# Two norms of a float32 transformer block: the first 128 tokens' tiles turned among the last output products, and two units begun ahead of the other tokens

## The reference

```python
def rmsnorm(x, w):
    y = x * lax.rsqrt(jnp.mean(x * x, axis=-1, keepdims=True) + EPS)
    return y * w

x = rmsnorm(x + (o * silu(gate)) @ odd_w_out, final_norm)   # end of first_block
h = rmsnorm(x, mix_norm);  proj = h @ w_mix_in              # 2048 -> 7184 columns, g_qkv first
...
x = x + attn @ w_xo                                         # the cross-attention's output
h = rmsnorm(x, ffn_norm);  u = causal_dwconv(h @ w_ffn_up, conv)
```

## Time and profile before

| | us |
|---|---|
| median of three runs | 2411.24 (2410.80 to 2411.55) |
| the profiled execution | 2411.45 |
| its span, first to last instruction | 2409.7 |
| PE busy | 2388.1 (99%) |
| PE weight loads busy | 2066.5 (86%) |
| DVE busy | 1629.7 (68%) |
| ACT busy | 1178.4 (49%) |
| weights read | 410.87 MB on the SP queue, 51.6% of the DMA engines' span |

### The profile page before, as it was taken

The page is one execution under the profiler, slowest core; times in us unless marked ns, Lnnn a source line. Parts: engine busy times, 40 slices in busy tenths (PEclk is TensorE's granted clock), DMA queues, the critical chain, the costliest instruction groups (busy, mean ns, idle before and its releaser), DMA issues.

```text
span 2409.7 us, 35511 instructions
## 1 busy us (share of the span) xinstructions
PE 2388.1 (99%) x14109; PEld 2066.5 (86%) x14109; DVE 1629.7 (68%) x2068; ACT 1178.4 (49%) x1439; POOL 157.9 (7%) x142
## 2 busy tenths in 40 slices
PE   8999999999999999999999999999999999999998
PEld 7888988898888888889988888988888888888887
DVE  6999776555685876696655446665777467755764
ACT  5433674544565654642654345545554334433433
POOL 1000000000200100000000000000212012200220
PEclk9999999999999999999999999999999999999999
DMA  8555546455436555553175555444565655555554
GB/s 251 189 195 186 164 140 214 147 180 171 158 108 207 166 183 177 183 167 106 37 253 176 199 186 164 141 175 161 190 203 179 208 175 194 189 194 191 183 180 143
DMA packets 337351, 422.45 MB, mean 175 GB/s; under 512 B 8494, under 2 KB 263228, under 8 KB 336716
## 3 DMA queue, kind: packets, MB, share of 16 engines
q1 hardware_dynamic: 334220, 410.87, 51.6%
q0 software_dynamic: 2544, 8.52, 1.1%
q10 hardware_dynamic: 464, 1.32, 0.2%
HBM read 418.53 MB, written 2.10 MB: 175 GB/s over the span
## 4 chain that ended last, share of the span: by engine, by line
PE 97%; DVE 1%; ACT 1%; DMA 0%; issue 0%; ACTq 0%; DVEq 0%
PE ps L759 36%; PE ps L760 18%; PE ps L816 10%; PE ps L818 10%; PE ps L817 10%; PE ps L763 1%; PE ps L764 1%; PE ps L762 1%; PE ps L1113 1%; PE ps L1105 1%; PE ps L1026 1%; PE ps L1030 1%; PE ps L855 0%; DVE h_cat L2343 0%; PE ps L1053 0%; DMA x<-in_x 0%
## 5 line engine op out<-in xcount | busy, mean ns | idle before, releaser
L759 PE MATMUL ps<-h_cat,w_hi 128*128 128x512 f32 x3824 | 1341.8, 396 | 5.4 <-DVE h_cat L2343 4.7
L760 PE MATMUL ps<-h_cat,w_lo 128*128 128x256 f32 x3824 | 1063.3, 278 | 0.0
L759 PEld LDWEIGHTS ps<-h_cat,w_hi 128*128 128x128 f32 x3824 | 717.0, 188 | 176.4 <-issue 8.3
L760 PEld LDWEIGHTS ps<-h_cat,w_lo 128*128 128x128 f32 x3824 | 719.4, 188 | 2.1 <-issue 1.9
L2200 DVE TENSOR_TENSOR w_lo<-ring,w_hi 128x2048 fp32r<-128x2048 f32 (+2 forms) x279 | 588.4, 2111 | 166.1 <-ACT w_hi L1417 163.1
L1417 ACT ACTIVATE w_hi<-ring 128x2048 fp32r<-128x2048 f32 (+2 forms) x279 | 493.0, 1767 | 87.6 <-PE ps L818 64.4
L2196 DVE TENSOR_TENSOR w_lo<-ring,w_hi 128x2048 fp32r<-128x2048 f32 (+1 forms) x136 | 302.8, 2232 | 231.2 <-ACT w_hi L1414 228.3
L1414 ACT ACTIVATE w_hi<-ring 128x2048 fp32r<-128x2048 f32 (+1 forms) x136 | 252.2, 1862 | 269.8 <-PE ps L818 239.6
L1435 ACT ACTIVATE stage<-ps 128x256 f32<-128x256 f32 x144 | 55.4, 384 | 400.1 <-PE ps L760 399.8
L816 PE MATMUL ps<-w_hi,h_cat 128*128 128x512 f32 x640 | 250.1, 391 | 0.0
L818 PE MATMUL ps<-w_hi,h_cat 128*128 128x512 f32 x640 | 249.2, 389 | 0.0
(11 more groups left out here) (466 smaller groups left out, 2335.2 us busy)
## 6 DMA issues: line engine op xcount, KB each, us to landing
ring<-in_w_ffn_up SPq DMA_DIRECT2D x44, 2048.0 KB, 8.0
ring<-in_w_mix_in SPq DMA_DIRECT2D x28, 2048.0 KB, 8.3
ring<-in_even_w_in SPq DMA_DIRECT2D x27, 2048.0 KB, 8.1
ring<-in_w_ffn_down SPq DMA_DIRECT2D x16, 2048.0 KB, 8.1
ring<-in_odd_w_in SPq DMA_DIRECT2D x11, 2048.0 KB, 9.3
ring<-in_even_w_out SPq DMA_DIRECT2D x8, 2048.0 KB, 8.2
ring<-in_odd_w_out SPq DMA_DIRECT2D x8, 2048.0 KB, 8.9
ring<-in_w_mix_out SPq DMA_DIRECT2D x8, 2048.0 KB, 8.2
```

The costliest lines, as they stand in the source:

```text
L759: mm(o[:, 0:2 * T], whi[slot][:, k, :], flat(cat[:, k]), start=first, stop=False)
L760: ins = mm(o[:, T:2 * T], wlo[slot][:, k, :], cat[:, k, 0, :], start=False, stop=end)
```

## The change

Behind norms 2 and 5 (`AHEAD`), and nowhere else:

- The eight transposes of the first tokens' first 1024 features move from behind the last output product to behind the second of the last four wide units of the second tokens.
- ACT, after the high parts of units 0 and 1, writes the first tokens' high parts of these eight tiles (`front_hi`, eight instructions of 128 columns), then unit 2's high part. DVE writes their low parts (`front_lo`, eight of 128 columns) after unit 0's low part.
- DVE makes unit 1's low part in two halves (`split_part`): contraction tiles 0 to 7 before `add_row`, which counts the new `lo_front`; tiles 8 to 15 behind the last `lo` of the norm, and only that counts `lo_ready`.
- PE, behind the last output product, runs `front_rows`: for units 0 and 1, eight matmuls each of the weights' high part with [high | low] of the first tokens (2 x 128 columns). Of the fillers three are left behind the mix norm and two behind the FFN norm, in other banks.
- Later `hi` and `lo` treat only the second tokens' 128 columns for pairs 0 to 3, and the first eight steps of units 0 and 1 multiply the high weights with the second tokens' 2 x 128 columns. Unit 1 starts on `lo_front` and waits for `lo_ready` at its ninth step.

The diff, without the list of semaphore names and most unchanged lines:

```diff
@@ -700,6 +700,9 @@
     HALVED = {1: 0, 2: 1, 5: 2}
+    AHEAD = {2: ("g_qkv", 0), 5: ("f_up0", 4)}
+    HALF_K = 8
+    FRONT, BACK = slice(0, P), slice(P, T)
@@ -728,7 +731,23 @@
-        def unit(g, j, n, i=None, rhs=None, tiles_ready=None, norm=None, read=None):
+        def two_of(o):
+            return o[:, 0:2 * T].rearrange("p (a t) -> p a t", a=2)
+        def front_rows(norm):
+            name, first = AHEAD[norm]
+            g = S[name]
+            pe.wait_ge(sem["half_ready"], first + 4)
+            for j in range(2):
+                before, at = seg_of_narrow[g.f0 + j - ACC]
+                pe.wait_ge(*emptied(before, at + 1))
+                pe.wait_ge(sem["hi_ready"], g.n0 + j + 1)
+                for k in range(HALF_K):
+                    mm(two_of(bank(g, g.n0 + j))[:, :, FRONT], whi[(g.n0 + j) % WHL][:, k, :], h_cat[:, k, :, FRONT],
+                       start=(k == 0), stop=False)
+        def unit(g, j, n, i=None, rhs=None, tiles_ready=None, norm=None, read=None, begun=None):
@@ -736,7 +755,11 @@
                 return
-            pe.wait_ge(*((sem["first_lo"], 1) if i is None and n == 0 else (sem["lo_ready"], k0 + 1)))
+            late_rest = begun is not None and j == 1
+            if late_rest:
+                pe.wait_ge(sem["lo_front"], AHEAD[begun][1] // 4 + 1)
+            else:
+                pe.wait_ge(*((sem["first_lo"], 1) if i is None and n == 0 else (sem["lo_ready"], k0 + 1)))
             if i is not None:
@@ -754,8 +777,13 @@
                         pe.wait_ge(sem["lo_ready"], 1)
+                if late_rest and step == HALF_K:
+                    pe.wait_ge(sem["lo_ready"], k0 + 1)
                 first, end = step == 0, step == g.kt - 1
-                if g.paired:
+                if begun is not None and step < HALF_K:
+                    mm(two_of(o)[:, :, BACK], whi[slot][:, k, :], cat[:, k, :, BACK], start=False, stop=False)
+                    ins = mm(o[:, T:2 * T], wlo[slot][:, k, :], cat[:, k, 0, :], start=False, stop=end)
+                elif g.paired:
                     mm(o[:, 0:2 * T], whi[slot][:, k, :], flat(cat[:, k]), start=first, stop=False)
@@ -780,7 +808,7 @@
                 unit(g, j, g.n0 + j, None, rhs, tiles_ready if j == 0 else None, norm if j == 0 else None,
-                     read if j == g.units - 1 else None)
+                     read if j == g.units - 1 else None, norm if norm in AHEAD and j < 2 else None)
                 if j == 0 and name in ("g_qkv", "x_k", "f_up0"):
@@ -821,7 +849,7 @@
-        def wide_seg(name, cat=None, tiles_ready=None, act0=None, first=0, norm=None, rows_apart=False, tile=None):
+        def wide_seg(name, cat=None, tiles_ready=None, act0=None, first=0, norm=None, rows_apart=False, tile=None, turned=None):
             g = S[name]
@@ -829,6 +857,9 @@
                         wide_unit(g, j, h_cat if cat is None else cat, tiles_ready, act0, (t,), tile=tile)
+                        if turned is not None and (t, j) == (1, g.units - 3):
+                            for p in range(4):
+                                turn_half(turned, p, 0).then_inc(sem["half_turned"], 1)
                 return
@@ -872,10 +903,13 @@
             if norm in HALVED:
-                for p in range(4):
-                    turn_half(norm, p, 0)
-                for n in range({1: 4, 2: 5, 5: 4}[norm]):
-                    mm(ps[n % 2][:, 0:T], ident[:], causal[:, 0:T], start=True, stop=True)
+                if norm in AHEAD:
+                    front_rows(norm)
+                else:
+                    for p in range(4):
+                        turn_half(norm, p, 0)
+                for n in range({1: 4, 2: 3, 5: 2}[norm]):
+                    mm(ps[n % 2 + (2 if norm in AHEAD else 0)][:, 0:T], ident[:], causal[:, 0:T], start=True, stop=True)
                 for p in range(4):
@@ -1092,7 +1126,7 @@
         pe.wait_ge(sem["masked"], A_ODD + DSA_HEADS)
-        wide_seg("o_out", tiles_ready=H_GROUPS["gate"], first=3, tile=gate_tile, rows_apart=True)
+        wide_seg("o_out", tiles_ready=H_GROUPS["gate"], first=3, tile=gate_tile, rows_apart=True, turned=2)
         turn_first(2)
@@ -1385,7 +1419,7 @@
         head_values(3)
-        wide_seg("x_out", tiles_ready=H_GROUPS["xattn"], first=2, rows_apart=True)
+        wide_seg("x_out", tiles_ready=H_GROUPS["xattn"], first=2, rows_apart=True, turned=5)
         turn_first(5)
@@ -1615,6 +1649,9 @@
             root_of(0, based, "half_std")
+            if k in AHEAD:
+                split_to(S[then].n0 + 2)
+                front_hi(k)
             split_to(S[then].n0 + 3)
@@ -1624,10 +1661,20 @@
             b = turned_tiles(k, p)
+            rows_ = slice(P if k in AHEAD and p < 4 else 0, T)
             for kk in range(2):
-                ins = af(h_hi[:, 2 * b + kk, :], turn_bank(k, p)[:, kk * T:(kk + 1) * T], ACT.Copy,
+                ins = af(h_hi[:, 2 * b + kk, rows_], turn_bank(k, p)[:, kk * T + rows_.start:(kk + 1) * T], ACT.Copy,
                          scale=col(NORMS[k], 2 * b + kk))
+        def front_hi(k):
+            for p in range(4):
+                act.wait_ge(sem["half_turned"], AHEAD[k][1] + p + 1)
+                for kk in range(2):
+                    ins = af(h_hi[:, 2 * p + kk, FRONT], turn_bank(k, p)[:, kk * T:kk * T + P], ACT.Copy,
+                             scale=col(NORMS[k], 2 * p + kk))
+                ins.then_inc(sem["half_hi"], 1)
@@ -1864,6 +1911,8 @@
         root_of(0, 3, "half_std", 1)
+        split_to(S["g_qkv"].n0 + 2)
+        front_hi(2)
         split_to(S["g_qkv"].n0 + 3)
@@ -2339,10 +2388,28 @@
             b = turned_tiles(k, p)
+            rows_ = slice(P if k in AHEAD and p < 4 else 0, T)
             for kk in range(2):
-                ins = stt(h_lo[:, 2 * b + kk, :], turn_bank(k, p)[:, kk * T:(kk + 1) * T], col(NORMS[k], 2 * b + kk),
-                          h_hi[:, 2 * b + kk, :].bitcast(F32), ALU.mult, ALU.subtract)
+                ins = stt(h_lo[:, 2 * b + kk, rows_], turn_bank(k, p)[:, kk * T + rows_.start:(kk + 1) * T], col(NORMS[k], 2 * b + kk),
+                          h_hi[:, 2 * b + kk, rows_].bitcast(F32), ALU.mult, ALU.subtract)
             ins.then_inc(sem["ht_ready"], 1)
+        def front_lo(k):
+            for p in range(4):
+                dve.wait_ge(sem["half_hi"], AHEAD[k][1] + p + 1)
+                for kk in range(2):
+                    ins = stt(h_lo[:, 2 * p + kk, FRONT], turn_bank(k, p)[:, kk * T:kk * T + P], col(NORMS[k], 2 * p + kk),
+                              h_hi[:, 2 * p + kk, FRONT].bitcast(F32), ALU.mult, ALU.subtract)
+                ins.then_inc(sem["half_ready"], 1)
+        def split_part(g, n, part_):
+            slot, c = n % WHL, g.c0 + (n - g.n0) // g.per_chunk
+            u0, k = ((n - g.n0) % g.per_chunk) * P, slice(8 * part_, 8 * part_ + 8)
+            dve.wait_ge(sem["hi_ready"], n + 1)
+            tt(wlo[slot][:, k, :], chunk(c % RING, g)[:, k, u0:u0 + P], whi[slot][:, k, :].bitcast(F32), ALU.subtract)\
+                .then_inc(sem["lo_ready" if part_ else "lo_front"], 1)
@@ -2392,7 +2459,12 @@
             scaled(k, x, 1)
-            split_to(S[then].n0 + 2)
+            if k in AHEAD:
+                split_to(S[then].n0 + 1)
+                front_lo(k)
+                split_part(S[then], S[then].n0 + 1, 0)
+            else:
+                split_to(S[then].n0 + 2)
             add_row(g, 1)
@@ -2415,6 +2487,10 @@
                 lo(k, b)
+            if k in AHEAD:
+                g = S[AHEAD[k][0]]
+                split_part(g, g.n0 + 1, 1)
+                st["split"] = g.n0 + 2
@@ -2724,7 +2800,9 @@
         scaled(2, x, 1)
-        split_to(S["g_qkv"].n0 + 2)
+        split_to(S["g_qkv"].n0 + 1)
+        front_lo(2)
+        split_part(S["g_qkv"], S["g_qkv"].n0 + 1, 0)
         add_row(S["o_out"], 1)
         two = lambda v: v.rearrange("p (a t) -> p a t", a=2)
```

More of the change, by code:

```diff
@@ L408, in build @@
              "row_ready", "emptied", "squared", "gained", "totalled", "std_ready", "rstd_ready", "scaled_dve", "scaled_act", "turned",
-             "scaled_one", "based", "half_std", "half_rstd", "ht_hi", "ht_ready", "tiles_read", "agate_read", "hhi_ready", "h_ready", "x_normed", "gain1_loaded", "gain_out_loaded",
+             "scaled_one", "half_turned", "half_hi", "half_ready", "lo_front", "based", "half_std", "half_rstd", "ht_hi", "ht_ready", "tiles_read", "agate_read", "hhi_ready", "h_ready", "x_normed", "gain1_loaded", "gain_out_loaded",
              "conv_tap", "bg_ready", "conv_total", "conv_mean", "conv_centred", "conv_sq", "conv_var", "conv_std", "conv_normed", "conv_silu",
```

## The result

The changed kernel takes 2422.3 us (median of five runs, 2421.97 to 2424.46) against 2411.55 us for the kernel before beside it (2410.80 to 2412.75): a ratio of 1.0046, with 95% between 1.0034 and 1.0059. It is slower by 10.8 us where 6.1 were forecast, and 0.3 us above the top of the predicted range. The profiled executions stand for this: spans of 2409.7 before and 2420.6 after, 10.9 more.

What follows compares the result with a forecast made beforehand. PE's chain bounds 97% of the span, so time is won only where PE idles or runs fillers. Stalls of 3.1 and 3.0 us, 6.1 together, on the median 2411.24 give 2417.3 us; range 2414.0 to 2422.0.

Steps and rivals of the forecast that it cites:

- The load behind the late half split: Load of units 4 and 5, issued 15 us later, delays unit 3: costs 3.1 us (mix norm) and 3.0 (FFN norm).
- The landing behind the mix norm: Load of units 4 and 5 takes the median 8.3 us from issue, landing at 809.6; earlier loads took 8.2 to 9.4.
- rival 2: ACT's table is loaded during the wait for the load: 1.28 us less at each norm, 2414.8 us; chance 0.20.
- The front parts: Work ahead of the first product and units 0 and 1: mostly hidden, each norm would win 1.0 us without the load.
- zero spare: DVE's low tiles and half split end at 788.3, when its add is due; at worst the add is 0.8 late.
- PE's gap ahead of the first product: Half as wide tiles behind the transposes save 0.4 us, so PE idles some 1.0 instead of 1.43.
- unit 1's 0.9: Eight steps of unit 1 shrink from 0.347 to 0.236 us; it runs free and gains the whole 0.9 us.
- The sum itself takes full speed: PE's clock in the stalls ahead of unit 3: the sum adds nothing for a fall to half speed.
- rival 3: The clock falls in a stall; one fall costs 2.8 us more, 2420, both at the upper end 2428; chance 0.12.
- The rows at the end: Clock falls between 2405 and 2406, over 3 us after PE's last matmul; a 3.8 us stall may or may not reach that.
- ACT's drains give the pitch of a unit: 5.54 us: Units of the loop behind the mix norm take 5.54 us each, 0.347 per step.
- rival 1: The late load is no bound and PE never waits for unit 1's bank; norms win 1.0 each: 2409.2; chance 0.07.

Runs made afterwards that it cites:

- experiment 1: Changed kernel with unit 1's low part made in one piece ahead of the last row's sum, so the load is on time: 2414.64 us, ratio 1.0014.
- experiment 2: Kernel before, with only the first load behind each norm waiting for one low part more: 2428.62 us, ratio 1.0072.
- experiment 5: Changed kernel, load still late, with ACT draining and DVE summing before they split in the two loops: 2415.52 us, ratio 1.0017.
- experiment 6: Experiment 4's kernel with the filler moved from behind unit 0 to behind unit 1: 2407.45 us; fillers at both: 2408.60; kernel before without filler: 2415.56.
- experiment 3: Changed kernel with ten fillers behind the mix norm and seven behind the FFN norm put ahead of unit 3: 2419.74 us, ratio 1.0034.
- experiment 4: Changed kernel with the second half split moved into DVE's gap behind the first scaling of the second tokens: 2413.63 us, ratio 1.0011.
- experiment 7: Experiment 1's kernel with the filler put behind unit 1 instead of unit 0: 2409.07 us, ratio 0.9990.
- experiment 8: Changed kernel with one more filler behind unit 3, of the mix loop (first kernel, 2422.63 us) or of both loops (second, 2422.82 us).

## Why the prediction was off, point by point

**Right: the direction and the mechanism.** "The load behind the late half split" happened at both norms as written: late count, late issue, ACT held in the split of unit 4 with its drain behind it, the sum late, PE idle ahead of unit 3, and no second stall. Experiments 1, 2 and 5 show the links: no late load, no stall; the late load alone, the stall; drain and sum ahead of the splits, none at unit 3.

**The terms of that step.** Against L', issue came at 12.8 and 12.0 (forecast 13.2 and 12.6). The landing behind the mix norm took 9.70, not 8.3, above the 9.4 at the top of the earlier trace rows; no run isolates why. Behind the FFN norm it took 8.2 (8.0). The table load did come after the landing, so rival 2 fell. Together unit 3 was 4.0 and 2.6 late, 6.6 for the 6.1 forecast. This term was sized well in sum, with a late landing at one norm against sooner issues at both.

**The front parts.** ACT's and DVE's narrow tiles took 0.27 each (2.16 and 2.17 for eight), not 0.30, and DVE stood 0.51 idle ahead of its add: "zero spare" was half a microsecond of spare. PE's gap ahead of the first product was 0.94 (1.0). Unit 0 ended at L' + 12.35, not 12.8, a gain of 0.6 rather than 0.1. With unit 1's 0.9 that makes about 1.5 a norm, 3.0 for two; experiment 6 collects 3.4.

**Wrong: the clock.** The step that failed is the clock in the stall, a term that the sum put at nothing: "The sum itself takes full speed", with a chance of 0.12 for rival 3. What the runs showed in its place: around waits of 4.90 and 3.64 us PE ran at half clock for 3.4 us each, 3.2 us together by the table. The rows at the end were read as leaving this open. A mean of 0.73 over the slice from 2405 puts the fall there near 2405.5, 3.6 us after PE's last matmul, and the stall forecast was 3.8; read so, they spoke for a fall. Rival 3's own price, half a unit or 2.8 us a fall, was too high against 1.6. Experiment 3, where filler products keep PE busy and the clock at 1.00, shows that idling was the cause. The Trainium skill ("TensorE: Matmul & The Clock Gate", section "Why this matters for your kernels"), set beside the sum, advises against idle gaps because the clock drops; the trace agrees with it at both stalls (0.66 over 5 us).

**Missing: the rhythm.** The second term that the sum put at nothing. "ACT's drains give the pitch of a unit: 5.54 us" was taken as a property of the unit. The runs show it to change with how PE entered the loop, and the prediction counted the filler behind unit 0 only as 0.46 us on the way. In the changed kernel the rhythm cost 2.1 us behind the mix norm and nothing behind the FFN norm, where the stall happened to leave PE in the fast one. The half-wide steps behind the filler matter too: with the stalls gone and nothing between them and the loop, both loops are slow (experiments 1 and 4). So an early load alone, as in rival 1, would not have brought its 2409.2: experiment 4 took 2413.6.

So 3.2 for the clock, 2.1 for the rhythm and 0.5 for the stalls, less 0.8 ahead of the change, make 5.0 of the 4.8 us between the forecast and the spans.

## What to carry to other kernels

Before work is moved behind the last step of a chain, look at what counts it: here half a split carried the semaphore that frees a load buffer, and an in-order engine that waits for that load holds back whatever is queued behind it. Price a stall of PE with the clock that it costs. And compare the pitch of a long loop of equal products before and after a change at its entry; if it moved, try one cheap product of another shape between the new entry and the loop, and measure: behind unit 1 it won 6.2 us (experiments 4 and 6), and the ten fillers of experiment 3 left the mix loop slow.

## What the hardware showed beyond that

- One sequence of instructions (a 512- and a 256-column matmul in turn, each with new weights) holds either of two rhythms: 346.7 or 353.3 ns per step at a granted clock of 1.00, for 20 to 30 units of 16 steps. A single filler between other shapes and the run was followed by the fast one in all eight loops profiled (the kernel before, experiments 6 and 7), and none by the slow one in all six (experiments 1 and 4, the kernel before without filler). What else breaks the run gives no such rule. Ten fillers were followed by the slow one (experiment 3). A wait of some 0.3 us ahead of unit 2 was followed by the fast one in experiment 5 and in the changed kernel, and by the slow one in the first kernel of experiment 8 (14 steps from 805.83 to 810.78, 354 ns each). A stall leaves either: in the changed kernel slow at the mix norm and fast at the FFN norm. Why there are two, no run shows.
- A product that computes nothing can be worth several times its price: at 0.46 us each, the kernel before is 4.7 us slower without its two.
- Half clock lasted 3.4 or 6.8 us around waits of 2.5 to 5.7 us. Twice it came with shorter ones: at a gap of 1.42 us ahead of the first product (experiment 2) that the kernel before passes at full clock with 1.43, and near the start of the kernel before without filler, at 14.9 us, behind a wait of 2.15, for 3.4 us.
